# Queries that carry their softmax scale, one engine for the normalisation, a shorter feed-forward loop, and another order ahead of the expert gathers

## The chip, the cores and the metric

The kernel runs on one core of one Trainium2 chip. The metric is the device time of one execution in microseconds (us), median of three runs. The engines of a core are TensorE (PE; its weight loads are PEld), VectorE (DVE), ScalarE (ACT), GpSimd (POOL) and SyncE (SP), and 16 DMA engines move data. Each engine works through a queue of its own in order; they meet only at semaphores.

## What is computed

Two transformer-like blocks of two layers each, on 256 tokens of width 1024, everything in float32. Cut to what bears on this change:

```python
# first block, for each of 2 layers
h = rms_norm(x, mix_pre_gain[l])            # 16 heads of 64, from h @ w_in[l]:
o_a = neighbourhood attention  (4 heads "na": scores * 64**-0.5 + bias, softmax)
o_b = latent attention         (4 heads "mla": scores * 96**-0.5, softmax)
o_c = axial-rope attention     (4 heads "ax": q, k rms-normed, scores * 64**-0.5, softmax)
o_d = sliding window with sink (4 heads "sw": scores * 64**-0.5, masked, softmax)
x = x + rms_norm(concat(o_a, o_b, o_c, o_d) @ w_out[l], mix_post_gain[l])
h = rms_norm(x, ffn_pre_gain[l])
u = conv over tokens (width 3) of h @ w_up[l]      # 1024 -> 2 * 2816
gate, val = split(u)
x = x + rms_norm((gelu(gate) * val) @ w_down[l], ffn_post_gain[l])

# second block, for each of 2 layers
xn = rms_norm_2(x, norm1_g[l])
x = x + mixing_sublayer(xn, ...)            # 6 stick-breaking heads, 6 mLSTM heads, 4 gating groups
xn = rms_norm_2(x, norm2_g[l])
q = xn @ peer_wq[l]                         # 8 heads, 2 sides, 128 wide
top 16 of 128 key scores on each side, top 16 of their 256 sums  -> idx, gate = softmax
x = x + sum over the 128 picks of a token of gelu(xn . u_tab[idx]) * gate * v_tab[idx]
```

The last line gathers, for each of 256 tokens, 128 rows of each of two tables (stored side by side, 8 KB a pick): 536.9 MB over both layers.

## The kernel before

**Splitting.** A float32 product is done as three products of parts: each operand is split into a high and a low part, high times high, high times low, low times high. These are the matmuls of L154, L155 and L156. ScalarE writes high parts by a cast, VectorE writes low parts by a subtraction.

**First block, attention (`mixing`).** Sixteen heads go through a pipeline in the order sw, mla, ax, na, four of each. For a head h, TensorE computes scores (256 by 256, as one PSUM bank of 128 x 512) in one of three `score_bank`s. VectorE's `scaled(h)` multiplies by the scale (L896) or, for the masked kinds na and sw, multiplies and adds the mask in one operation, both into the tile `s_sb` in SBUF, then takes the negated row maximum (L898). ScalarE takes two exps from `s_sb`, with sums (L764), into `p_sb`. VectorE's `probs(h)` takes the reciprocal of the sums (L911) and multiplies the first token half by it (L913), while GpSimd multiplies the second half (L705). TensorE's `turn(h)` waits for both (semaphores `att_probs` and `att_probs_pool`) and transposes the probabilities (L1022), then multiplies them with v. TensorE's scores for head h wait until VectorE has scaled head h-3, since that frees the bank. Before that, GpSimd computes the reciprocal root for the axial q and k in one helper call, and ScalarE copies the latent queries (`lat_up`).

**First block, feed-forward (`gated_ffn`).** 22 chunks j of w_up and w_down. For a chunk TensorE does up(j) (two halves of the sequence of products into banks 4 and 5), ScalarE takes u to SBUF (L466), VectorE convolves (L526), ScalarE takes the gelu (L476), VectorE gates and splits the product (L534 to L539), TensorE does down(j) into four banks that collect over all chunks. ScalarE (L448, L454) and VectorE (L510) split the loaded weights, in two buffers each. TensorE's order is up(1); then a loop of ten turns with up, down, up, down; and at the end up(22), down(21), down(22). `pe_early` (L403) raises the two counts that let ScalarE write the first weight parts; it runs behind the out product of attention. `sp_early` issues the first two loads of w_up (L380), of w_down and of the convolution's parameters; SyncE runs it (L1107) behind its wait for all values of attention. `after_mix` is the norm behind attention's out product (L227), and `mid` the norm ahead of the feed-forward. In ScalarE's and VectorE's queues the splits of the first weights (`act_early`, `dve_early`) stand ahead of both.

**Second block (`mixing_out`).** The end of the mixing sublayer for token half 1 is interleaved with the choice of experts for token half 0. The orders are written out by hand, one list of calls for each engine: TensorE L2039 to L2076, ScalarE L2145 to L2171, VectorE from L2350. Names: `turn_x` (L1992) transposes the normed tokens, `take_x` copies the transposes to SBUF, `queries` (L2015, 32 matmuls of 128x128 in one row of the timeline) and `key_scores` compute the choice's scores; `first_choice` (L2260) takes the top 16 of each side, `second_choice` (L2278) the top 16 of the sums, `numbers` (from L2294) the table rows, whose last instruction writes `picked`. `sb_values` and `ml_rows`, `ml_probs`, `ml_values` (L1950) belong to the stick-breaking and mLSTM heads; `magnitudes` and `logs` (Ln, and so a table load on ScalarE, L1757) belong to the stick-breaking weights. `y_squares`, `y_sums` (L2203), `y_root` (L165, GpSimd), `y_scaled` (L2217) norm the head outputs; `out(1, n)` is the out product of token half 1. GpSimd issues the gathers (L1938), each one row of picks (8 KB into each of 128 partitions, 1 MB) into a ring of slots. The first four slots are free early (they wait for the values of the heads); numbers 5 to 8 wait for out(1, 0), the others for out(1, 1). Then, row by row, VectorE forms the dot product (L2326), the diagonal (L2336), and TensorE adds the row (L2034).

## Time and profile before

| | |
|---|---|
| median of 3 runs | 2390.38 us (2387.23 to 2391.78) |
| profiled execution | 2389.33 us, of which the span is 2387.6 us |
| busy: TensorE | 2072.4 us (87%) |
| busy: VectorE | 1749.7 us (73%) |
| busy: ScalarE | 843.5 us (35%) |
| busy: GpSimd | 698.4 us (29%) |
| moved by DMA | 700.50 MB, mean 293 GB/s |
| mean granted clock of TensorE | 0.953 |

Of the span, the first block takes up to about 690 us (layer 1 up to 345), the second block the rest. In the second block, each layer begins with some 170 us of mixing and ends with a gather phase of about 620 to 650 us, in which the DMA engines are the busiest. Times in the rows below are microseconds from the start of the span. A row of a timeline tells the start, the duration, the engine, the line, the operation with its tiles and shapes, and how many instructions it joins; in brackets the idle time of the engine just ahead of it, and what ended that. A granted clock of 1.00 is TensorE's full 2.4 GHz, 0.50 is 1.2 GHz.

### The profile page before, as it was taken

Reading aid. Unit: us, or ns where it says so; the run is one execution under the profiler, and the core shown is the slowest. Engines: PE = TensorE matmul, PEld = TensorE weight load, DVE = VectorE, ACT = ScalarE, POOL = GpSimd, SP = SyncE. Lnnn points to the kernel's source line nnn. Section 1 sums busy time; section 2 is a strip of 40 time slices with the busy share of each in tenths; the row PEclk is TensorE's granted clock in tenths of the full one; section 3 lists DMA queues with packets and bytes.
Section 4 is the critical chain, followed back from the end, with each engine's and each line's share of the span. In section 5 each row is a group of like instructions: output and inputs, shape, how many; then the busy total and the mean of one; then the engine's idle time right before and its main releaser. Section 6 shows DMA issues by size and latency. Waiting matters only on the chain. (4 is left out here: it accounts for less than half of the span.)

```text
span 2387.6 us, 28061 instructions
## 1 busy us (share of the span) xinstructions
PE 2072.4 (87%) x8698; PEld 1341.1 (56%) x8698; DVE 1749.7 (73%) x4213; ACT 843.5 (35%) x2074; POOL 698.4 (29%) x631
## 2 busy tenths in 40 slices
PE   8999999999979889898878777699899997777776
PEld 6779977679969765454333332298745542332232
DVE  6857777677767667778787787576676778787875
ACT  6656655666647521111111111176211211111110
POOL 1200001200001044444444444110243444444441
PEclk9999999999989889999999999998799999999999
DMA  6254533335535359999999999754399999999996
GB/s 220 80 214 180 187 120 91 120 135 186 186 132 165 124 205 420 419 421 421 422 421 421 421 421 422 266 156 150 131 421 419 421 421 421 421 422 421 421 422 269
DMA packets 138668, 700.50 MB, mean 293 GB/s; under 512 B 14392, under 2 KB 40248, under 8 KB 66872
## 3 DMA queue, kind: packets, MB, share of 16 engines
q0 software_dynamic: 73728, 536.90, 54.3%
q1 hardware_dynamic: 64824, 162.22, 19.5%
q8 instruction: 52, 0.85, 0.1%
q14 instruction: 64, 0.52, 0.1%
HBM read 698.03 MB, written 1.05 MB: 293 GB/s over the span
## 5 line engine op out<-in xcount | busy, mean ns | idle before, releaser
L2034 PE MATMUL bank<-ARENA 128*128 128x512 f32 x2048 | 990.5, 630 | 219.2 <-DVE ARENA L2336 218.4
L2034 PEld LDWEIGHTS bank<-ARENA 128*128 128x128 f32 x2048 | 385.4, 198 | 802.9 <-DVE ARENA L2336 432.0
L2326 DVE CUSTOM_DVE_ANT_0 ARENA<-ARENA 128x1024 f32<-128x1024 f32 x512 | 626.2, 1223 | 271.6 <-DMA ARENA<-in_uv_rows,ARENA 264.5
L1938 POOL DMA_INDIRECT ARENA<-in_uv_rows,ARENA x512 | 586.4, 1145 | 710.8 <-PE bank L2034 638.6
L154 PE MATMUL bank<-PARTS,PARTS 128*128 128x256 f32 (+4 forms) x1488 | 488.5, 328 | 17.6 <-DVE PARTS L539 7.0
L155 PE MATMUL bank<-PARTS,PARTS 128*128 128x256 f32 (+6 forms) x1552 | 497.5, 321 | 0.0
L156 PE MATMUL bank<-PARTS,PARTS 128*128 128x256 f32 (+6 forms) x1552 | 497.1, 320 | 0.0
L2142 ACT ACTIVATE ARENA<-ARENA 128x1 f32<-128x1 f32 x512 | 104.0, 203 | 1049.0 <-DVE ARENA L2326 1048.3
L154 PEld LDWEIGHTS bank<-PARTS,PARTS 128*128 128x128 f32 x1488 | 286.7, 193 | 42.4 <-DVE PARTS L284 7.4
L155 PEld LDWEIGHTS bank<-PARTS,PARTS 128*128 128x128 f32 (+2 forms) x1552 | 298.5, 192 | 16.7 <-issue 1.0
L156 PEld LDWEIGHTS bank<-PARTS,PARTS 128*128 128x128 f32 (+2 forms) x1552 | 298.0, 192 | 17.0
L2336 DVE TENSOR_SCALAR ARENA<-CON,ARENA 128x128 f32<-128x128 f32 x512 | 176.7, 345 | 10.1 <-ACT ARENA L2142 5.1
L213 POOL TENSOR_SCALAR STAT<-STAT 128x1 f32<-128x1 f32 x8 | 4.5, 565 | 450.4 <-ACT ARENA L207 450.4
L526 DVE SCALAR_TENSOR_TENSOR ARENA<-ARENA 128x255 f32<-128x255 f32 x176 | 77.4, 481 | 79.5 <-ACT ARENA L470 71.2
L2015 PE MATMUL bank<-ARENA 128*128 128x128 f32 (+1 forms) x704 | 121.7, 334 | 0.0
L2015 PEld LDWEIGHTS bank<-ARENA 128*128 128x128 f32 x704 | 111.2, 203 | 17.7 <-issue 9.9
L504 DVE TENSOR_TENSOR PARTS<-ARENA,PARTS 128x512 fp32r<-128x512 f32 x176 | 109.5, 686 | 9.1 <-ACT PARTS L448 9.1
L448 ACT CAST PARTS<-ARENA 128x512 fp32r<-128x512 f32 x176 | 95.9, 629 | 10.6 <-PEq L403 10.4
L1341 DVE TENSOR_TENSOR PARTS<-ARENA,PARTS 128x384 fp32r<-128x384 f32 (+2 forms) x160 | 72.4, 485 | 36.9 <-ACT PARTS L1337 36.7
L335 DVE TENSOR_TENSOR PARTS<-ARENA,PARTS 128x512 fp32r<-128x512 f32 (+2 forms) x112 | 67.6, 635 | 28.5 <-ACT PARTS L331 28.1
L1337 ACT CAST PARTS<-ARENA 128x384 fp32r<-128x384 f32 (+2 forms) x160 | 68.9, 460 | 32.9 <-PE bank L156 31.0
L331 ACT CAST PARTS<-ARENA 128x512 fp32r<-128x512 f32 (+2 forms) x112 | 61.7, 578 | 42.5 <-PE bank L156 40.9
(258 smaller groups left out, 1919.2 us busy)
## 6 DMA issues: line engine op xcount, KB each, us to landing
ARENA<-in_w_up_tiles SPq DMA_DIRECT2D x44, 1024.0 KB, 5.9
ARENA<-in_w_down SPq DMA_DIRECT2D x44, 512.0 KB, 3.7
ARENA<-in_w_out SPq DMA_DIRECT2D x32, 512.0 KB, 4.2
ARENA<-in_wq_tiles SPq DMA_DIRECT2D x16, 1024.0 KB, 11.8
ARENA<-in_w_in SPq DMA_DIRECT2D x40, 384.0 KB, 3.6
ARENA<-in_w_in SPq DMA_DIRECT2D x24, 512.0 KB, 10.5
ARENA<-in_w_in SPq DMA_DIRECT2D x40, 256.0 KB, 2.9
ARENA<-in_uv_rows,ARENA POOLq DMA_INDIRECT x512, 22.5
```

What stands on the lines that cost most here:

```text
L154: mm(out_ap, w_hi, x_hi, start=start, stop=False, skip_group_check=True)
L155: mm(out_ap, w_lo, x_hi, start=False, stop=False, skip_group_check=True)
L156: return mm(out_ap, w_hi, x_lo, start=False, stop=stop, skip_group_check=True)
L448: nc.scalar.copy(up_hi[s][u], up_raw[s][:, u, :]).then_inc(s_("up_hi"), 1)
L504: nc.vector.tensor_tensor(up_lo[s][u], up_raw[s][:, u, :], up_hi[s][u], ALU.subtract).then_inc(s_("up_lo"), 1)
L526: last = nc.vector.scalar_tensor_tensor(c[:, to], u[:, frm], w, c[:, to], ALU.mult, ALU.add)
L1938: nc.gpsimd.indirect_dma_start(out=slot[i % SLOTS], out_offset=None, in_=table[:, :], in_offset=bass.IndirectOffsetOnAxis(ap=picked[:, t, ...
L2015: last = mm(to, w[:, k, :], x, start=(k == 0), stop=(k == KD - 1), skip_group_check=True)
L2034: last = mm(row_banks[t][n][:, :], diag[i % N_DIAG], slot[i % SLOTS][:, D + n * 512:D + (n + 1) * 512], start=(c == 0), stop=(c == NPICK - ...
L2142: nc.scalar.activation(gelu_dots[:, t, c:c + 1], dots[:, t, c:c + 1], ACT.Gelu_apprx_tanh).then_inc(S("gelu_ready"), 1)
L2326: v.tensor_tensor_reduce(u, u, xn[:, t, :], 1.0, 0.0, ALU.mult, ALU.add, dots[:, t, c:c + 1]).then_inc(S("dots_ready"), 1)
L2336: v.tensor_scalar(diag[i % N_DIAG], ident, gelu_dots[:, t, c:c + 1], gate[:, t, c:c + 1], ALU.mult, ALU.mult).then_inc(S("diagonal_ready"), 1)
```

## The change

1. *Attention.* The scale goes with the queries: the reciprocal root of the axial q is taken with `64 * eps` and an unscaled sum of squares, which makes it 64^-0.5 times as large (one more operation on GpSimd), and ScalarE multiplies the latent queries by 96^-0.5 where it copied them. The eight heads without a mask lose their scaling operation on VectorE; their maximum and their exps read the PSUM bank. VectorE multiplies both halves of the probabilities, GpSimd none, and TensorE waits for VectorE alone. The scores of head h wait for the exps of head h-3 where that one has no mask.
2. *Feed-forward.* The buffers of w_up and w_down are laid out anew. The first w_up loads are issued right behind SyncE's wait for all scores, the w_down loads where they were. The loop is one turn shorter, and the order at the end is up(20), down(19), up(21), up(22), down(20), down(21), down(22). The splits of the last w_down move: ScalarE's behind taking u(22), VectorE's behind the convolution of 22.
3. *Second block.* Three orders change: TensorE does ml_rows(4) ahead of turn_x(0) and sb_values(2), (3) behind key_scores(0); ScalarE does logs(4) ahead of take_x(0); VectorE does first_choice(0) ahead of ml_probs(4) and second_choice(0) ahead of y_sums(1).

```diff
-            up_raw_at, up_at = at, at + 4096
-            down_raw_at, down_at = at + 12288, at + 14336
+            up_raw_at, up_at = at + 12288, at + 4096
+            down_raw_at, down_at = at, (at + 16384, at + 2048)
...
-            def sp_early(sp):
+            def sp_up_early(sp):
                 for s in range(2):
                     load_up(sp, s, s)
+
+            def sp_down_early(sp):
+                for s in range(2):
                     load_down(sp, s, s)
...
-                with pe.Fori(0, NF // 2 - 1) as it:
+                with pe.Fori(0, NF // 2 - 2) as it:
                     up(1, it * 2 + 2)
                     down(0, it * 2 + 1)
                     up(0, it * 2 + 3)
                     down(1, it * 2 + 2)
+
+                up(1, NF - 2)
+                down(0, NF - 3)
+                up(0, NF - 1)
                 up(1, NF)
+                down(1, NF - 2)
                 down(0, NF - 1)
                 down(1, NF, stop=True)
...
                     gelu(s, j + 1)
+                    if j + 2 < NF:
+                        act_split_down(act, 1 - s, j + 2, 16 * ((j + 1) // 2 + 1))
                     if j + 1 < NF:
-                        act_split_down(act, 1 - s, j + 2, 16 * ((j + 1) // 2 + 1))
                         take_u(1 - s, j + 2, j + 1)
...
                     if j == NF - 2:
                         fill(act, 4, 6)
+                        act_split_down(act, 1 - s, NF, 16 * (NF // 2))
...
-                dve_split_down(dve, 1, NF)
                 fill(dve, 0, 4)
                 convolve(1, NF, NF - 1)
+                dve_split_down(dve, 1, NF)
                 gated(1, NF)
...
-                    pool_rstd(pool, STAT[:, 16:28], 1.0 / HD, 12).then_inc(s_("ax_rstd"), 1)
-                    for h in range(NHD):
-                        pool.wait_ge(s_("att_recip"), h + 1)
-                        nc.gpsimd.tensor_scalar(p_sb[:, h % 3, 1, :], p_sb[:, h % 3, 1, :], sums[:, h, 1:2], None,
-                                                ALU.mult).then_inc(s_("att_probs_pool"), 1)
+                    nc.gpsimd.tensor_scalar(ssC[:, :, 0:4], ssC[:, :, 0:4], 1.0, HD * EPS, ALU.mult, ALU.add)
+                    nc.gpsimd.tensor_scalar(ssC[:, :, 4:6], ssC[:, :, 4:6], 1.0 / HD, EPS, ALU.mult, ALU.add)
+                    pool.drain()
+                    nc.gpsimd.tensor_tensor(ssC, ssC, view(HALF[:, 0:12], (6, NT), (1, 6)), ALU.pow).then_inc(s_("ax_rstd"), 1)
...
-                        nc.scalar.copy(qb[:, t, :], bank[t][:, 0:384])
+                        nc.scalar.mul(qb[:, t, :], bank[t][:, 0:384], 96 ** -0.5)
...
-                            last = nc.scalar.activation(p_sb[:, h % 3, t, :], s_sb[:, h % 3, t, :], ACT.Exp,
+                            frm = s_sb[:, h % 3, t, :] if masked[h] else score_bank[h % 3][:, t * T:(t + 1) * T]
+                            last = nc.scalar.activation(p_sb[:, h % 3, t, :], frm, ACT.Exp,
...
-                        else:
-                            nc.vector.tensor_scalar(s, frm, sc, None, ALU.mult).then_inc(s_("att_scaled"), 1)
-                        dve.drain()
+                            s = s_sb[:, h % 3, :, :]
+                            dve.drain()
                         last = nc.vector.tensor_reduce(nmax[:, h, :], s, AX, ALU.max, negate=True)
...
-                        nc.vector.reciprocal(sums[:, h, :], sums[:, h, :]).then_inc(s_("att_recip"), 1)
-                        dve.drain()
-                        nc.vector.tensor_scalar(p_sb[:, h % 3, 0, :], p_sb[:, h % 3, 0, :], sums[:, h, 0:1], None,
-                                                ALU.mult).then_inc(s_("att_probs"), 1)
+                        nc.vector.reciprocal(sums[:, h, :], sums[:, h, :])
+                        dve.drain()
+                        for t in range(NT):
+                            last = nc.vector.tensor_scalar(p_sb[:, h % 3, t, :], p_sb[:, h % 3, t, :], sums[:, h, t:t + 1],
+                                                           None, ALU.mult)
+                        last.then_inc(s_("att_probs"), 1)
...
-                        if h >= 3:
-                            pe.wait_ge(s_("att_scaled"), h - 2)
+                        if h >= 3 and masked[h - 3]:
+                            pe.wait_ge(s_("att_scaled"), masked_until[h - 3])
+                        elif h >= 3:
+                            pe.wait_ge(s_("att_exp"), h - 2)
...
-                        pe.wait_ge(s_("att_probs_pool"), h + 1)
...
                                  ).then_inc(S(f"mix_post_{l}"), 16)
+                    up_down.sp_up_early(sp)
                     sp.wait_ge(*mixed.all_values)
-                    up_down.sp_early(sp)
+                    up_down.sp_down_early(sp)
...
+                    ml_rows(pe, 4)
                     turn_x(0)
-                    sb_values(2)
-                    sb_values(3)
-                    ml_rows(pe, 4)
                     queries(0)
                     suffix_sums(pe, 4)
                     key_scores(0)
+                    sb_values(2)
+                    sb_values(3)
                     ml_scores(pe, 4)
...
                     magnitudes(act, 4)
+                    logs(act, 4)
                     take_x(0)
                     ml_weight(act, 4)
-                    logs(act, 4)
...
+                    first_choice(0)
                     ml_probs(4)
-                    first_choice(0)
+                    second_choice(0)
                     y_sums(1)
-                    second_choice(0)
                     numbers(0)
```

## Rows read from the trace of the kernel before

**Rows 1.** The page's slices: GB/s moved by DMA, 40 slices of 59.7 us

```profile
GB/s 220 80 214 180 187 120 91 120 135 186 186 132 165 124 205 420 419 421 421 422 421 421 421 421 422 266 156 150 131 421 419 421 421 421 421 422 421 421 422 269
```

**Rows 2.** GpSimd's timeline: start, us, engine, line, tiles, count, [idle, its releaser]

```profile
853.58 2.91 POOL L165 TENSOR_TENSOR STAT<-STAT,HALF 128x16 f32<-128x16 f32 x1
...
860.45 1.21 POOL L1938 DMA_INDIRECT ARENA<-in_uv_rows,ARENA  x1 [3.96 <-DVE ARENA L2310]
...
872.90 1.38 POOL L1938 DMA_INDIRECT ARENA<-in_uv_rows,ARENA  x1 [7.51 <-PE bank L156]
```

**Rows 3.** Table by stage, 874 to 875: engines' busy us, granted clock, DMA share, GB/s

```profile
874.00:875.00 1.00, 1.00 (x6) 0.80 (x6) 0.92 (x2) 0.00 (x0) 0.70 (x2) 1.00 0.23 49
```

**Rows 4.** VectorE's timeline before the first layer's gathers

```profile
847.31 0.48 DVE L2260 MAX8 ARENA<-ARENA 128x8 f32<-128x128 f32 x2
...
850.87 1.22 DVE L2203 TENSOR_REDUCE STAT<-ARENA 128x16 f32<-128x1024 f32 x1 [0.29 <-ACT ARENA L2096]
...
853.06 0.42 DVE L2278 MAX8 ARENA<-ARENA 128x8 f32<-128x256 f32 x1
...
855.81 0.17 DVE L2294 TENSOR_SCALAR ARENA<-ARENA 128x16 uint32<-128x16 uint32 x1
...
859.40 0.16 DVE L2217 TENSOR_TENSOR STAT<-STAT 128x6 f32<-128x6 f32 x1
```

**Rows 5.** TensorE's timeline, second block, and one row of the table by stage

```profile
828.78 1.97 PE L1992 MATMUL bank<-CON,ARENA 128*128 128x128 f32 x8 [1.58 <-DVE ARENA L2247]
...
836.42 6.69 PE L2015 MATMUL bank<-ARENA 128*128 128x128 f32 x32
...
846.53 3.79 PE L1950 MATMUL bank<-ARENA 128*128 128x65 f32 x32
...
882.38 3.73 PE L2015 MATMUL bank<-ARENA 128*128 128x128 f32 x32
...
829.00:842.00 13.00, 13.00 (x55) 11.64 (x55) 2.31 (x4) 3.64 (x7) 0.00 (x0) 0.50 0.00 0
...
1690.86 5.77 PE L1950 MATMUL bank<-ARENA 128*128 128x65 f32 x32
```

**Rows 6.** ScalarE's timeline, second block, first layer

```profile
827.39 0.63 ACT L1752 ACTIVATE ARENA<-ARENA 128x512 f32<-128x512 f32 x1
...
837.69 1.28 ACT L1757 ACT_TABLE_LOAD   x1
```

**Rows 7.** Timeline of three engines, end of the first feed-forward

```profile
332.35 1.12 ACT L454 CAST PARTS<-ARENA 128x512 fp32r<-128x512 f32 x2
...
333.89 1.30 DVE L510 TENSOR_TENSOR PARTS<-ARENA,PARTS 128x512 fp32r<-128x512 f32 x2
...
337.11 0.59 ACT L466 COPY ARENA<-bank 128x512 f32<-128x512 f32 x1 [3.64 <-PE bank L156]
...
340.97 0.43 DVE L534 TENSOR_TENSOR ARENA<-ARENA 128x256 f32<-128x256 f32 x1 [0.48 <-ACT ARENA L476]
...
342.32 0.50 PE L154 MATMUL bank<-PARTS,PARTS 128*128 128x512 f32 x1 [2.50 <-DVE PARTS L539]
```

**Rows 8.** ScalarE's and VectorE's timeline behind attention; the L380 loads' time to landing

```profile
135.20 4.27 ACT L448 CAST PARTS<-ARENA 128x512 fp32r<-128x512 f32 x8 [5.21 <-PEq L403]
...
DMA to landing us min/median/max: 4.9/4.9/4.9
...
141.88 2.72 DVE L227 TENSOR_TENSOR ARENA<-bank,ARENA 128x512 f32<-128x512 f32 x4
```

**Rows 9.** Groups by form, 78 to 112: busy us, mean ns, idle before, releasers

```profile
L705 POOL TENSOR_SCALAR ARENA<-ARENA,STAT 128x256 f32<-128x256 f32 x14 | 14.9, 1062 | 36.9 <-DVE STAT L911 36.9
...
L1022 PE MATMUL bank<-CON,ARENA 128*128 128x128 f32 x52 | 8.3, 282 | 1.7 <-POOL ARENA L705 0.9 <-issue 0.8
...
L896 DVE TENSOR_SCALAR ARENA<-bank 128x512 f32<-128x512 f32 x8 | 5.5, 689 | 0.6 <-PE bank L156 0.6
...
L913 DVE TENSOR_SCALAR ARENA<-ARENA,STAT 128x256 f32<-128x256 f32 x14 | 5.0, 354 | 1.3
```

More of the change, by code:

```diff
@@ L369, in gated_ffn @@
             up_lo = [[parts(up_at + (4 * s + u) * 1024 + 512, 512) for u in range(4)] for s in range(2)]
-            down_hi = [[parts(down_at + (2 * s + u) * 1024, 512) for u in range(2)] for s in range(2)]
-            down_lo = [[parts(down_at + (2 * s + u) * 1024 + 512, 512) for u in range(2)] for s in range(2)]
+            down_hi = [[parts(down_at[s] + u * 1024, 512) for u in range(2)] for s in range(2)]
+            down_lo = [[parts(down_at[s] + u * 1024 + 512, 512) for u in range(2)] for s in range(2)]
             g_hi = [parts(g_at + s * 512, T) for s in range(2)]
@@ L678, in mixing @@
                 nsink = STAT[:, 104:108]
-                scale_of = {"na": HD ** -0.5, "mla": 96 ** -0.5, "ax": HD ** -0.5, "sw": HD ** -0.5}
+                masked = [kind in ("na", "sw") for kind, *_ in heads]
+                masked_until = [sum(masked[:h + 1]) for h in range(NHD)]
                 score_bank = [bank[6], bank[7], bank[1]]
@@ L1043, in projected @@
                             if n == 0:
-                                pe.wait_ge(s_("att_scaled"), NHD - 1)
+                                pe.wait_ge(s_("att_scaled"), masked_until[NHD - 2])
                             if n < KD:
```

14 lines of the change are left out of this document (6 added, 8 removed).

## The prediction

> **What bounds the kernel now.** I read four views in this order. First the page's forty slices: from slice 16 to 25, and from 30 to the end, the DMA engines move 420 GB/s without a dip [rows 1]. These are the two gather phases of the second block (512 rows of 1 MB); nothing the change does alters their bytes, so each phase lasts as long as before and only its start can move. Second, GpSimd's timeline before the phase: the first gather goes out at 860.45 us, directly behind VectorE's write of `picked`, three follow it, and the fifth waits until 872.90 for out(1,0) on TensorE [rows 2]. Between them DMA falls to a share of 0.23 at 874 [rows 3]. So a microsecond won on the chain to the gathers is a microsecond won at the end, if the second batch moves along with the first. Third, the timelines of the three engines on that chain. Fourth, the first block: it has no transfer bound. TensorE sets its pace except in a few named gaps, so only those gaps can be won.
>
> **Part 1, VectorE order before the gathers.** In the kernel before, VectorE runs first_choice(0) (from 847.31), then y_sums(1) (850.87), second_choice(0) (853.06) and numbers(0) (855.81), whose last instruction writes `picked` at 859.49, just as y_scaled(1) begins (859.40) [rows 4]. y_sums(1) waited for TensorE's last values. The change puts second_choice(0) in front of y_sums(1). It lasts from 853.06 to the start of numbers(0) at 855.81, 2.75 us, and now runs while TensorE finishes the values, provided that the key scores come early enough (part 2 sees to that). After y_sums only numbers(0) is left: 859.49 − 855.81 = 3.7 us, of which 0.4 is a pause. GpSimd's y_root(1) stands ahead of the gathers in its queue: it begins 0.1 us behind y_sums and its pow ends at 856.49 [rows 2], 3.4 us after y_sums, so the two finish together. I take **2.9 us** a layer (2.75, plus the pause that overlaps), between 2.4 (GpSimd last) and 3.1. y_scaled(1) moves by as much, so out(1,0) and the second batch do too.
>
> **Part 2, TensorE order before the gathers.** Before: turn_x(0) at 828.78 after 1.58 us idle; sb_values(2), (3) from 830.55; ml_rows(4); queries(0) at 836.42, 6.69 us long; then values(2 to 4) as 32 matmuls from 846.53 to 850.15 [rows 5]. ml_rows(4) now fills the idle 1.6 us ahead of turn_x(0), and queries(0) follow turn_x directly. The cover that is gone: sb_values hid the copies of the turned x. ScalarE takes its half behind logs(4), which brings a table load ahead of it: magnitudes end at 828.0 and a load is 1.28 us [rows 6]; with 0.63 for the Ln and 0.59 for the copy that is 830.6; VectorE's half ends at about the same time. That is a bubble of 0.9 us. Net, the same matmuls end 0.7 us earlier at equal clock. The order also decides what waits: ml_probs(4) now stands behind first_choice(0) on VectorE, and ml_values(4), sb_values(4) wait for it. first_choice lasts 3.4 us, and over that time TensorE has sb_values(2), (3) (1.8 us at 2.4 GHz) and ml_scores(4) (1.8) to do, then ml_values(2), (3): covered.
> The unknown is the granted clock. From 829 to 842 it is 0.50, that is 1.2 GHz, after the 1.6 us of idle [rows 5]. With ml_rows(4) in the gap the engine is idle 0.4 and 0.9 us instead. At full clock a group of 32 query matmuls lasts 3.7 us (at 882.38), against 6.69 [rows 5], and turn_x 1.0 against 1.77. Working the whole chain at 2.4 GHz, y_squares' last part ends at 844.1 and y_sums starts then, not at 850.87: 6.7 us. With the clock falling where it falls now, y_sums starts at 848.5: 2.3 us. The second layer shows a third course: in its 32 value matmuls the clock fell with the engine busy, and they took 5.77 us, not 3.79 [rows 5]. The change puts 48 such narrow matmuls almost together. I take this middle course, the clock full through queries(0) and lost in the values: 6.7 − 1.9 = **4.8 us** in the first layer, and 7.1 − 1.9 = 5.2 in the second, where the present chain is 0.4 longer. Bounds a layer: −4.5 (all of it at half clock) to 7.1.
> A rule speaks against the order on ScalarE. The row shows the Ln starting 1.29 us after its table load starts, hence 1.28 a load [rows 6]. The Trainium skill, "ScalarE: Activation LUTs", section "What ACT_TABLE_LOAD costs", gives about 2.66 us for each switch, drain included. By it the copy of x, and the gathers, would come 1.4 us later a layer; the trace disagrees, so the row's figure stands.
> Sum of parts 1 and 2: 7.7 + 8.1 = **15.8 us**.
>
> **Part 3, the end of the feed-forward.** Before, the order is up(22), down(21), down(22). ScalarE takes u at 337.11, VectorE convolves, ScalarE takes the gelu, VectorE gates from 340.97, and TensorE idles 2.50 us until 342.32 [rows 7]. A down product lasts 2.75 us (twelve matmuls, 0.229 apart). Now down(20) comes behind up(22), so up(22) ends at 334.15 and two down products, until 339.65, cover the chain. But the split of the last w_down is moved into that chain: ScalarE may start it only when down(20) is done (337.1), 1.12 us for two casts, and the gelu stands behind it (338.3); VectorE splits from 337.8 in 1.3 us, then gates 1.35 us. Those durations are in [rows 7]. Product 22 can start at 340.5, a gap of 0.8 us. Gain 2.5 − 0.8 = 1.7 us a layer, **3.4 us**, from 0 to 5.0. up(22) is needed 2.75 us earlier; its low parts are written about 5 us before its present start, so it doesn't wait.
>
> **Part 4, earlier loads of w_up.** They move from the last values to the last scores, 14 us earlier. VectorE's post-norm starts at 141.88, 2.6 us after TensorE is done, because the splits of w_up precede it; that looks like a late load. It isn't: ScalarE's first cast at 135.20 was released by TensorE's sequencer at L403, `pe_early`, which the change leaves where it is, and the load issued at 125.44 had landed 4.9 us later, at 130.3, so ScalarE (idle from 129.98) had it [rows 8]. **0 us**. In between there is nothing that queues behind the two loads on SyncE's queue but the w_down loads, which start when they did.
>
> **Part 5, attention.** Per head without a mask VectorE loses a 512-wide scale from PSUM (0.69, with its drain 0.78 us) [rows 9]; every head gets a second 256-wide multiply (0.27 from start to start, 0.35 long [rows 9]). GpSimd's half took 1.06 us and released the transposes; the second multiply ends 0.44 us sooner (0.27 + 0.35 behind the first's start) [rows 9]. But TensorE is at its own pace: in 78 to 112 us it waited 1.7 us ahead of its transposes [rows 9], so 1.7 is the most to win a layer. Following the heads: the first two come 0.5 earlier, the MLA and axial ones run at TensorE's 2.34 and 2.50 us, the four neighbourhood heads keep their masked scale, get 0.27 us each and need 2.8 to 3.1 us of VectorE, so lag returns at the end. I take 0.6 a layer, **1.2 us**, from −0.5 to 1.7 each. The max and exps now read PSUM: the PSUM-reading L896 takes 689 ns [rows 9], the 512-wide SBUF reduction 686, so 0. The Trainium skill, "VectorE: DVE Perf Modes", section "The TRN2 errata", lists 62 more cycles for a PSUM source, an estimate of 0.065 us on eight heads a layer, 0.5 us; the two rows don't show it. The epsilon operation added on GpSimd (0.35 us) has 3.4 us until VectorE needs its result: 0.
>
> **Sum.** 15.8 + 3.4 + 0 + 1.2 = 20.4 us off the profiled execution: span 2387.6, whole 2389.3, so 2368.9. The median of the runs is 1.05 above the profiled one: **2370.0**.
>
> **Rivals.** *The clock stays at 2.4 GHz through the chain*: 9.6 + 10.0 in parts 1 and 2, 24.2 in all, 2366.2; the hole in DMA [rows 3] may close as well, about 1.2 us a layer, down to 2363. For it: the idle is shorter. Against: the narrow matmuls. *The clock falls ahead of queries(0), as now*: 5.2 + 5.0, 14.8 in all, 2375.6. For it: both layers did so. *The early loads do count*: post-norm starts at once, 2.2 us a layer more, 2365.6; [rows 8] speak against it. *The gathers don't follow the chain* (the parts' gains are lost in the waits between batches): 4.6 in all, 2385.8; the unbroken 420 GB/s speaks against it. *Slower*: with queries and 48 narrow matmuls in one piece, TensorE is held at 1.2 GHz from turn_x(0) through out(1,0). y_sums then starts 4.5 us later, less 2.9 for part 1, and out(1,0)'s 24 matmuls, 0.427 us apart instead of 0.227, take 10.2 us where 13 slow ones among them make 8.0 now: 3.8 later a layer, 7.6 against 4.6 won elsewhere: 2393.4. It decides from 2.3 us of lateness a layer on, about 11 us more at half clock than now.
>
> **How the numbers follow.** Forecast 0.36, clock stays 0.20, clock falls as now 0.24, loads count 0.05, gathers don't follow 0.07, slower mechanism 0.06, and 0.02 for things unseen. Two runs within 0.2% (4.8 us) can hardly be told apart. Faster by more: 0.36 + 0.20 + 0.24 + 0.05 + 0.01 = 0.86. Within: 0.07 + 0.03 of the slower case (it lies at +3) = 0.10. Slower by more: 0.04. The range takes the first four cases and the bounds of parts 3 and 5 (about ±2): 2362 to 2380.
>
> **What would show it.** First gathers at about 849 and 1695 on the old time axis, less what came before, with second_choice ahead of y_sums; granted clock 1.00 through queries(0) and 0.50 in the values; a gap near 0.8 us ahead of the last down product; ScalarE's first w_up cast still released by L403, with the post-norm 2.6 us behind TensorE. Wrong if the clock follows another course (±5 us), or if the start of the gathers moves and the end doesn't.

## The result, and the profile after

The changed kernel took **2375.69 us** (median of 5 runs, 2373.18 to 2378.83) against 2390.24 (5 runs) before: ratio 0.9943, interval 0.9929 to 0.9957, 14.6 us faster. In a second comparison it took 2379.38 (5 runs, 2374.26 to 2383.57) against 2390.27: ratio 0.9948, 0.9935 to 0.9962, 10.9 us faster. The profiled execution is one at 2378.83 us, span 2376.7, 10.9 us less than the span before. The forecast was 2370.0, a gain of 20.4, in a range of 2362 to 2380. So sign and range held, and part of the gain didn't come: 5.8 us of 20.4 by the first comparison, 9.5 by the second and by the profiled execution.

"Half clock" below is a granted clock of 0.50; a figure between 0.50 and 1.00 is the mean over a stretch that has both. First, the two slice rows of the page after the change, TensorE's granted clock and DMA's GB/s (40 slices of 59.4 us):

```profile
PEclk9999999999989889999999999998799999999989
...
GB/s 221 114 171 181 185 136 86 131 124 185 185 142 166 124 231 419 420 421 421 421 421 421 421 421 421 261 156 151 153 420 419 421 421 421 421 421 421 421 421 268
```

The gather phases are as they were, 420 GB/s from slice 16 to 25 and again from slice 30 on: only their start moved. So the question is where 10.9 us came from ahead of them. Subtracting the same instruction's start in the two traces gives this ledger. A minus sign is a gain.

| up to | shift of the start | gained in this stretch | forecast |
|---|---|---|---|
| last transposes of attention, layer 0 (121.01 to 120.53) | −0.48 | −0.5 | −0.6 |
| norm behind feed-forward 0 (345.37 to 344.26) | −1.11 | −0.6 | −1.7 |
| last transposes of attention, layer 1 (463.12 to 461.36) | −1.76 | −0.65 | −0.6 |
| norm behind feed-forward 1 (688.67 to 685.36) | −3.31 | −1.55 | −1.7 |
| turn_x(0), second block, layer 0 (828.78 to 825.44) | −3.34 | 0 | 0 |
| y_sums(1) (850.87 to 846.78) | −4.09 | **−0.75** | **−4.8** |
| first gather (860.45 to 853.31) | −7.14 | **−3.05** | −2.9 |
| end of the gather phase (1538.36 to 1530.63) | −7.73 | −0.6 | 0 |
| turn_x(0), layer 1 (1674.72 to 1668.74) | −5.98 | +1.75 | 0 |
| y_sums(1), layer 1 (1697.19 to 1690.04) | −7.15 | **−1.17** | **−5.2** |
| first gather, layer 1 (1706.63 to 1696.43) | −10.20 | **−3.05** | −2.9 |
| end of the gather phase (2380.71 to 2369.86) | −10.85 | −0.65 | 0 |

The row that failed is TensorE's chain from turn_x to y_sums. Its timeline in the first layer, which answers to [rows 5]:

```profile
825.44 1.97 PE L2007 MATMUL bank<-CON,ARENA 128*128 128x128 f32 x8 [0.20 <-DVE ARENA L2262]
...
828.24 5.73 PE L2030 MATMUL bank<-ARENA 128*128 128x128 f32 x32 [0.83 <-issue]
...
835.55 1.90 PE L1965 MATMUL bank<-ARENA 128*128 128x64 f32 x16
...
839.13 7.09 PE L1965 MATMUL bank<-ARENA 128*128 128x65 f32 x32
...
855.07 1.10 PE L1988 MATMUL bank<-CON,ARENA 128*128 128x128 f32 x8 [2.49 <-DVE ARENA L2238]
```

Turn_x is reached after 0.20 us of idle time instead of 1.58, as meant, and the bubble ahead of queries(0) is 0.83 us (0.9 in the forecast). But turn_x (1.97 us) and most of queries(0) (5.73 us, against 3.73 at full clock [rows 5]) run at half clock, and the 32 value matmuls take 7.09 us, twice their 3.79 [rows 5]. In the second layer it is the same:

```profile
1682.39 7.09 PE L1965 MATMUL bank<-ARENA 128*128 128x65 f32 x32
```

The table by stage shows why; the columns after the length are busy time and number for PE, PEld, DVE, ACT, POOL, then granted clock, DMA share and GB/s:

```profile
832.00:839.00 7.00, 6.94 (x54) 6.58 (x53) 3.32 (x17) 1.28 (x3) 0.00 (x0) 0.98 0.01 2
...
839.00:846.00 7.00, 7.00 (x34) 6.93 (x34) 3.47 (x13) 0.80 (x2) 0.00 (x0) 0.51 0.00 0
...
825.00:870.00 45.00, 39.69 (x200) 35.64 (x199) 28.56 (x99) 12.09 (x30) 10.59 (x9) 0.73 0.30 107
```

From 832 to 839 TensorE was busy 6.94 of 7.00 us at a clock of 0.98, and in the next seven it was busy throughout and had 0.51. So the clock fell in unbroken work: ahead of the fall stood the 64-wide sb_values (835.55) and ml_scores(4), whose matmuls use 64 rows. The same stretch of 45 us in the kernel before, and then, for each of the two kernels, the chain from turn_x to y_sums alone (before, after):

```profile
825.00:870.00 45.00, 35.49 (x203) 31.57 (x204) 23.96 (x83) 12.67 (x30) 7.69 (x7) 0.73 0.16 59
...
828.78:850.87 22.09, 22.03 (x121) 20.18 (x122) 6.88 (x23) 7.59 (x14) 0.00 (x0) 0.69 0.00 1
```

```profile
825.44:846.78 21.34, 20.45 (x114) 19.64 (x115) 9.23 (x34) 6.72 (x14) 0.00 (x0) 0.66 0.00 1
```

0.73 over the 45 us in both, and on the chain itself 0.69 before and 0.66 after: 13.6 us at half clock before, in one piece in turn_x to queries(0) (828.9 to 842), and 14.5 after, in two pieces (turn_x and queries(0), then the values). In the second layer it is 15.1 and 14.5. So the new order took no half clock off this chain, it only moved it from some of the work to other work. What is left is the 0.7 us that the prediction gave the order at equal clock (ml_rows(4) off the chain, the bubble on it): 0.75 was measured.

VectorE and GpSimd behind it (answering to [rows 4] and [rows 2]):

```profile
840.18 0.42 DVE L2293 MAX8 ARENA<-ARENA 128x8 f32<-128x256 f32 x1
...
846.78 1.22 DVE L2218 TENSOR_REDUCE STAT<-ARENA 128x16 f32<-128x1024 f32 x1 [3.94 <-ACT ARENA L2111]
...
848.96 0.17 DVE L2309 TENSOR_SCALAR ARENA<-ARENA 128x16 uint32<-128x16 uint32 x1
...
852.11 0.23 DVE L2325 TENSOR_SCALAR ARENA<-ARENA 128x16 uint32<-128x16 f32 x1
```

```profile
849.49 2.91 POOL L165 TENSOR_TENSOR STAT<-STAT,HALF 128x16 f32<-128x16 f32 x1
...
853.31 1.21 POOL L1953 DMA_INDIRECT ARENA<-in_uv_rows,ARENA  x1 [0.91 <-DVE ARENA L2325]
...
866.02 1.20 POOL L1953 DMA_INDIRECT ARENA<-in_uv_rows,ARENA  x1 [7.70 <-PE bank L156]
```

second_choice(0) (840.18) is done while TensorE works on the values. From the start of y_sums (846.78) to the first gather (853.31) it is now 6.53 us instead of 9.58: 3.05 us, in both layers. GpSimd's pow ends at 852.40 and VectorE's last instruction ends at 852.34, so they finish together, as forecast.

ScalarE's order (answering to [rows 6]):

```profile
824.73 1.28 ACT L1772 ACT_TABLE_LOAD   x1
...
826.03 0.63 ACT L1772 ACTIVATE ARENA<-ARENA 128x512 f32<-128x512 f32 x1
...
826.59 0.59 ACT L2129 COPY ARENA<-bank 128x512 f32<-128x512 f32 x1
```

The Ln starts 1.30 us after its table load, and the copy of x comes 0.56 us later: the row's 1.28 us held, not the 2.66 us of the Trainium skill ("ScalarE: Activation LUTs", section "What ACT_TABLE_LOAD costs").

The tail of the first feed-forward (answering to [rows 7]): ScalarE's split of the last w_down, and the first matmul of down(22).

```profile
338.00 1.14 ACT L463 CAST PARTS<-ARENA 128x512 fp32r<-128x512 f32 x2 [0.42 <-PE bank L156]
...
341.21 0.50 PE L154 MATMUL bank<-PARTS,PARTS 128*128 128x512 f32 x1 [0.58 <-DVE PARTS L550]
```

The gap ahead of down(22) is 0.58 us instead of 2.50, in the second layer too: 1.92 us each (forecast 1.7). Behind attention (answering to [rows 8]):

```profile
134.72 4.27 ACT L457 CAST PARTS<-ARENA 128x512 fp32r<-128x512 f32 x8 [5.21 <-PEq L407]
...
141.40 2.71 DVE L227 TENSOR_TENSOR ARENA<-bank,ARENA 128x512 f32<-128x512 f32 x4
```

The first cast of w_up is still released by TensorE's sequencer, 5.21 us late, and the norm starts 0.48 us earlier, by what attention won, no more: the early loads gave nothing. And attention, 78 to 112 us (answering to [rows 9]):

```profile
L1036 PE MATMUL bank<-CON,ARENA 128*128 128x128 f32 x53 | 8.9, 287 | 1.1 <-DVE ARENA L925 1.0
...
L925 DVE TENSOR_SCALAR ARENA<-ARENA,STAT 128x256 f32<-128x256 f32 x28 | 8.6, 350 | 1.1
...
L909 DVE TENSOR_REDUCE STAT<-bank 128x2 f32<-128x512 f32 x8 | 5.5, 687 | 1.6 <-PE bank L156 1.6
```

VectorE multiplies 28 halves at 350 ns each; TensorE waited 1.1 us ahead of its transposes instead of 1.7; the maximum read from PSUM takes 687 ns, from SBUF 686. The 62 more cycles that the Trainium skill ("VectorE: DVE Perf Modes", section "The TRN2 errata") gives a PSUM source don't show.

What ate the first block's gain in these two traces is the clock again. Rows before and after of the first product of the feed-forward, and before of the last down product of the second layer:

```profile
153.00:157.00 4.00, 3.98 (x33) 4.00 (x34) 2.23 (x6) 1.52 (x5) 0.00 (x0) 1.00 0.07 23
...
685.00:689.00 4.00, 3.63 (x10) 2.33 (x8) 0.33 (x1) 0.33 (x1) 0.00 (x0) 0.57 0.00 0
```

```profile
153.00:157.00 4.00, 4.00 (x23) 4.00 (x22) 1.72 (x5) 1.02 (x3) 0.00 (x0) 0.57 0.01 4
```

Behind the norm, the stretch at half clock lasted until 153 before and until 156.4 after: 1.3 us lost, and 1.8 in the second layer (until 494 and until 498). This is not the change's doing as far as the other traces show: the old first block stands unchanged in e1, e5 and e6 below, and its stretch lasts 3.4 or 6.8 us there (3.4 and 3.4, 3.4 and 6.8, 6.8 and 3.4 in the two layers); the new one stands in e4, e7, e8, e9 and e12, with 6.8 and 6.8, three times 6.8 and 3.4, and 3.4 and 3.4. On the other side, the 2.5 us gap in the second layer's tail was followed by 3.4 us at half clock (0.57 over 685 to 689); in the trace after there is none, a gain of 1.4 us that the forecast didn't have. In all the traces together, such a stretch follows the gap in five of ten places where the gap is 2.5 us (before, e1, e3, e5, e6, two layers each) and in none of 18 where it is 0.58, so closing the gap wins this part on average, not each time.

### The profile page after: what moved, and what is told of

It is laid out like the page before. It is cut to its first block and busy times, and to the rows that moved or that the text cites. A ratio compares the mean times of both kernels' runs of the same rounds, so it can differ in the third digit from the quotient of the medians.

```text
span 2376.7 us, 27988 instructions
## 1 busy us (share of the span) xinstructions
PE 2080.6 (88%) x8693; PEld 1345.2 (57%) x8698; DVE 1747.3 (74%) x4229; ACT 842.3 (35%) x2074; POOL 659.2 (28%) x601
```

## The experiments

**Each part alone, and the whole once more.** Four kernels; the kernel before took 2390.27 us in this comparison.

The second block's three orders alone:

```diff
  kernel before, and of the change only:
+                    ml_rows(pe, 4)
                     turn_x(0)
-                    sb_values(2)
-                    sb_values(3)
-                    ml_rows(pe, 4)
                     queries(0)
...
+                    logs(act, 4)
                     take_x(0)
...
+                    first_choice(0)
                     ml_probs(4)
+                    second_choice(0)
                     y_sums(1)
```

> The kernel before with the new orders of the second block alone (TensorE, ScalarE, VectorE). Theory A, the trace of the changed kernel read as it stands: from the write of y_sums to the first gather 3.05 us a layer are won (second_choice out of the way), from turn_x to y_sums only 0.75 and 1.17 us, because the granted clock falls again in the value matmuls; the hole in DMA shrinks by 0.6 us a layer. Sum 3.8 + 0.6 + 4.2 + 0.6 = 9.2 us faster: about 2381. In its trace the 32 value matmuls last near 7.1 us in both layers (3.79 and 5.77 before). Theory B, the fall in the values was an accident of that one execution, as the place of a clock fall moves with all that runs ahead of it: then at least one layer shows the 32 value matmuls in under 5.8 us, and the gain is 11 to 16 us.

Measured: 2380.29 us, ratio 0.9961 (0.9948 to 0.9973), 10.0 us faster; theory A had said 9.2. queries(0) and the values:

```profile
833.68 5.68 PE L2015 MATMUL bank<-ARENA 128*128 128x128 f32 x32 [0.83 <-issue]
...
844.54 7.09 PE L1950 MATMUL bank<-ARENA 128*128 128x65 f32 x32
```

7.09 us to the hundredth, and in the second layer too; turn_x to y_sums takes 21.31 us in both. With the changed kernel's two traces and that of e10, the values last 7.09 us eight times in eight, so this fall goes with the program's order and theory B falls.

The feed-forward alone (its hunks of the diff, unchanged):

> The kernel before with the feed-forward's part alone (buffers, early w_up loads, one turn less, new order at the end). Theory A: the gap ahead of the last down product shrinks from 2.50 to 0.6 us in both layers, 3.8 us in all, and the loads give nothing (ScalarE's first w_up cast is still released by TensorE's sequencer): about 2386. Theory B: closing the gap also keeps the clock up in the last product of the second feed-forward (at half speed in the kernel before from 685 to 689), 1.5 us more: about 2385. Rival: the loads count, post-norm starts at once, 8 us faster.

Measured: 2385.88 us, ratio 0.9980 (0.9971 to 0.9989), 4.4 us faster, between A's 3.8 and B's 5.3. There is no stretch at half clock in the last product in its trace (3.10 us of VectorE's idle time ahead of the norm, not 4.55), as B says. But the next experiment keeps the gap of 2.5 us, and its trace has no such stretch either (3.10 us), so one trace doesn't decide between A and B. The rival, that the loads count, falls.

Attention alone:

> The kernel before with the attention's part alone (scale in the queries, VectorE normalises both halves). Theory A: 0.5 to 0.65 us a layer, 1.1 us in all, about 2389, which the comparison can hardly tell from no change; in the trace the last transposes of probabilities stand 0.5 us earlier in the first layer and 1.1 us in the second. Rival: the shift by 0.5 us changes where the clock falls ahead of the feed-forward (3.4 us at half clock behind the transposes of the norm before, 6.8 us in the changed kernel), then attention alone is 1.3 us a layer slower there and the kernel is 1.5 us slower than before in all.

Measured: 2391.10 us, ratio 1.0001 (0.9992 to 1.0009): no change. The last transposes come 0.61 and 1.44 us earlier, as theory A has it, but turn_x(0) comes at 828.89 (828.78 before): the gain is gone between the norm behind feed-forward 1 and turn_x, where 41 us ran at half clock and not 24. That isn't the attention's doing, since e4 shows the same two figures for two executions of one program. The rival's place (149 us) was wrong, with 3.4 us at half clock there, as before.

The whole:

> The changed kernel again. Its first profiled execution was 3.1 us above its own median. Theory A (the clock's course is set by the program): the same stretches at half clock as in the first trace, 6.8 us from 149 on and 17 us between turn_x and out(1,0), values at 7.1 us. Theory B (it differs from execution to execution): other lengths, and the span differs by that: per 3.4 us at half clock on the chain, 1.7 us of time. Ratio to before 0.994 either way.

Measured: 2379.38 us; the profiled execution took 2383.57. Theory A held on the chain from turn_x to y_sums: queries(0) 5.63, values 7.09, 21.31 us in all. The 6.8 us at half clock from 149 came again too, but e9, with the same first block, has 3.4 there. But its turn_x(0) is at 829.29, 3.9 us later than in the first trace, with the norm behind the feed-forward at 685.52 (685.36). One row of each between the two, first this kernel, then the first trace:

```profile
795.00:813.00 18.00, 16.66 (x71) 13.26 (x71) 13.48 (x34) 15.39 (x33) 3.11 (x2) 0.53 0.66 259
```

```profile
795.00:813.00 18.00, 13.87 (x69) 10.80 (x69) 15.94 (x38) 16.67 (x38) 3.11 (x2) 0.72 0.58 229
```

0.53 against 0.72. Between 686 and turn_x this execution had 41 us at half clock, the first trace 24. So theory B holds for the stretches ahead of turn_x: they differ between executions of one program. The traces of e7, e8, e9 and e12, whose programs are the changed kernel up to turn_x, have 31 to 34 us there. This costs the one execution 3.7 us against the other, and so it is a large part of what can spread the changed kernel's ten runs over 10 us; only two of the ten left a trace.

Sum of the parts: 10.0 + 4.4 − 0.8 = 13.6, between the whole's 14.6 and 10.9. They add up.

**Which order gives what.** VectorE's order alone on the kernel before (only the first_choice and second_choice lines of the diff above):

> The kernel before with VectorE's new order alone (first_choice ahead of ml_probs(4), second_choice ahead of y_sums(1)); TensorE and ScalarE as before. Theory A (part 1 of the forecast is worth its 3 us only because TensorE brings the key scores earlier): first_choice starts no earlier, so ml_probs(4), which TensorE waits for, moves back behind it, and second_choice pushes y_sums back; picked is no earlier, and y_scaled(1) with the second batch is as late or later: 0 to 3 us slower a layer, 2390 to 2396. Theory B (the 3 us are VectorE's own): first gather 3 us earlier a layer, 2384.

Measured: 2385.88 us, ratio 0.9982 (0.9973 to 0.9991), 3.9 us faster. Theory A falls, and B's 6 us is too much:

```profile
853.78 3.68 PE L1950 MATMUL bank<-ARENA 128*128 128x65 f32 x16 [0.68 <-DVE ARENA L2192]
...
858.01 1.22 DVE L2203 TENSOR_REDUCE STAT<-ARENA 128x16 f32<-128x1024 f32 x1 [1.72 <-ACT ARENA L2096]
```

y_sums to the first gather is 6.82 us (9.58 before), so the 2.8 us are VectorE's own. But y_sums comes 23.30 us behind turn_x, not 22.09: TensorE waits 0.68 us for ml_probs(4), and 16 of its values run at half clock. From turn_x to the first gather that is net 1.5 and 1.9 us a layer.

TensorE's and ScalarE's orders alone (the other two hunks):

> The kernel before with TensorE's and ScalarE's new orders alone; VectorE as before. Theory A: from turn_x to y_sums 0.8 to 1.2 us less, the 32 value matmuls at half clock (7.1 us); VectorE's first_choice is done in time, but second_choice stays behind y_sums, so the first gather gains only that: 1 us a layer and some 0.3 of the hole, 2388. Theory B: the two orders are worth their sum only together (9.2 us), and this one alone nothing: 2390. Either way the values last 7.1 us.

Measured: 2385.04 us, ratio 0.9985 (0.9976 to 0.9993), 4.7 us faster.

```profile
843.91 6.50 PE L1950 MATMUL bank<-ARENA 128*128 128x65 f32 x32
```

Values 6.50 us, turn_x to y_sums 20.75 (1.3 to 1.7 less than before), y_sums to the gather 9.58 as before. Neither theory: it is worth about as much as VectorE's order, and within the intervals the two add up (3.9 + 4.7 = 8.6, of 10.0).

**What lets the clock fall in the values.** First, sb_values(2), (3) put back between turn_x and queries in the changed kernel:

```diff
                     turn_x(0)
+                    sb_values(2)
+                    sb_values(3)
                     queries(0)
                     suffix_sums(pe, 4)
                     key_scores(0)
-                    sb_values(2)
-                    sb_values(3)
                     ml_scores(pe, 4)
```

> The changed kernel with sb_values(2), (3) back between turn_x(0) and queries(0), all else as changed. Theory N (the clock falls in the values because 16 narrow value matmuls and the narrow ml_scores stand right ahead of them): the 32 value matmuls last 3.8 us again, and y_sums would come 3.3 us earlier but for VectorE, which gets the key scores about 1 us later and has 6.9 us of work ahead of y_sums: from turn_x to y_sums 19.7 to 20.5 us instead of 21.3, 1 to 1.6 us a layer faster than the changed kernel. Rival R (the clock falls a fixed time after turn_x, whatever the order): values at 7.1 us again, and the kernel the same or 1 us a layer slower than the changed one. Rival S (with sb_values there the half clock of the start lasts 13.7 us, as in the kernel before): queries(0) at 6.5 us, values 3.8, turn_x to y_sums about 22.3 us, 1 us a layer slower.

Measured: 2373.92 us, ratio 0.9931 (0.9913 to 0.9949).

```profile
840.62 2.00 PE L1965 MATMUL bank<-ARENA 128*128 128x65 f32 x16
...
843.54 3.68 PE L1965 MATMUL bank<-ARENA 128*128 128x65 f32 x16 [0.92 <-DVE ARENA L2207]
```

Half of the values ran full (2.00 us for 16), half at half clock. Turn_x to y_sums is 21.84 us, 0.5 more than in the changed kernel; the first half clock lasted 10.2 us. None of the three came out as written: the second fall came 17.0 us behind turn_x and not 13.7, which refutes a fixed time, and it came behind ml_scores and 16 values, so that narrow work precedes it here as well. It came inside the 0.92 us in which TensorE waited for VectorE, though, so that here a wait is as near a cause as the narrow work. The time can't be told from the changed kernel's.

Next, matmuls of zeros, 512 wide in bf16, whose result nobody reads, added to the changed kernel's work:

```diff
                     turn_x(0)
+                    wide(bank[2], 3)
                     queries(0)
                     suffix_sums(pe, 4)
                     key_scores(0)
+                    wide(bank[0], 2)
                     sb_values(2)
+                    wide(bank[0], 2)
                     sb_values(3)
+                    wide(bank[0], 4)
                     ml_scores(pe, 4)
```

where wide(to, n) is n times `matmul(to, ZERO[:, 0:P], ZERO[:, :])`.

> The changed kernel with 512-wide bf16 matmuls of zeros, whose result nobody reads, set between the steps: 3 behind turn_x(0), 2 ahead of sb_values(2), 2 ahead of sb_values(3), 4 ahead of ml_scores(4). At full clock they take 0.22 us each, 1.8 us for the eight. Theory N (narrow work lets the clock fall): the clock stays full through the values (3.8 us instead of 7.1), turn_x to y_sums is 21.3 + 1.8 + 0.4 - 3.3 = 20.2 us, 1 us a layer faster than the changed kernel. Rival R (the fall comes at a fixed time after turn_x, or from something else): the values stay near 7 us and y_sums is 2 us or more later: 2 to 4 us a layer slower.

Measured: 2368.46 us, ratio 0.9915 (0.9901 to 0.9930).

```profile
825.92 1.49 PE L2056 MATMUL bank<-ZERO 128*128 128x512 bf16 x3
...
827.20 3.86 PE L2030 MATMUL bank<-ARENA 128*128 128x128 f32 x32
...
837.89 3.79 PE L1965 MATMUL bank<-ARENA 128*128 128x65 f32 x32
```

The three fill the 0.83 us bubble and overrun it by 0.24 (at half clock they take 1.3 us), queries(0) run full, and so do the values: 18.07 us from turn_x to y_sums instead of 21.34, and 17.91 instead of 21.30 in the second layer. Theory N's sign is right, its sum too small, since it had not seen the first stretch shrink (6.8 to 3.4 us). Then the eight without the three:

> The changed kernel with the eight 512-wide matmuls of zeros behind key_scores(0) alone (2, 2 and 4, around the narrow value matmuls), without the three behind turn_x(0). With all eleven, turn_x to y_sums was 18.07 us instead of 21.34, queries(0) 3.86 instead of 5.73, the values 3.79 instead of 7.09. Theory N (each fall answers to the narrow work right ahead of it): the first stretch at half clock is 6.8 us again and queries(0) 5.6 to 5.8, the values stay at 3.8, turn_x to y_sums is 19.5 to 20 us: some 1.5 us a layer faster than the changed kernel. Rival (the first stretch sets the second): with the first as long as before, the values fall again, 7 us, and the eight cost their 1.8: 2 us a layer slower than the changed kernel.

Measured: 2375.95 us, ratio 0.9938 (0.9925 to 0.9952).

```profile
826.59 5.61 PE L2030 MATMUL bank<-ARENA 128*128 128x128 f32 x32 [0.83 <-issue]
...
839.03 5.67 PE L1965 MATMUL bank<-ARENA 128*128 128x65 f32 x32
```

Values 5.67 and 5.08 us, turn_x to y_sums 21.47 and 21.01: the eight alone win on the values what they cost. Theory N falls in this form, the rival holds more of it. And the three without the eight:

> The changed kernel with the three 512-wide matmuls of zeros behind turn_x(0) alone, without the eight. Of the four combinations, none and the eight alone have the first stretch at half clock 6.8 us long (queries(0) 5.6 to 6.2 us) and turn_x to y_sums 21.0 to 21.5 us, all eleven 3.4 us long, queries(0) 3.86 and 18.07 us. Theory P (the three set the first stretch, and with it the rest): queries(0) at 3.9 us, the values at 3.8 without the eight too, turn_x to y_sums 16.3 us; about 2366. Theory N' (the three shorten the first stretch, the narrow work ahead of the values still lets the clock fall a second time): queries(0) 3.9, values 5.5 to 7.1, turn_x to y_sums 18.2 to 19.8: about 2370. Rival (the three alone do nothing): queries(0) 5.7, 21.3 us, as the changed kernel.

Measured: 2368.54 us, ratio 0.9914 (0.9900 to 0.9928).

```profile
827.02 3.86 PE L2030 MATMUL bank<-ARENA 128*128 128x128 f32 x32
...
836.04 5.78 PE L1965 MATMUL bank<-ARENA 128*128 128x65 f32 x32
```

Theory N': queries 3.86 us (4.59 in the second layer, where the 3.4 us at half clock reach into them), the values 5.78 and 5.04, turn_x to y_sums 18.39 and 17.73. Of the four combinations, none gives 21.34, the eight 21.47, the three 18.39, all 18.07: **three dummy matmuls in a wait of 0.83 us are worth 3 us a layer, and the eight nothing.** The times agree: 2368.54 and 2368.46 us with the three, 2375.69, 2379.38 and 2375.95 without. Shown is thus that the half clock behind turn_x answers to how TensorE fills the bubble. Not settled is the fall in the values: with the eight wide ones ahead of them it still came (e9), and with the three besides it did not. Narrow work stood ahead of each of these falls, but narrow work alone doesn't decide, and no run sets wide work of the computation itself in its place.

**The early loads.** In the changed kernel, the release of the w_up buffers ahead of the last ten units of attention's out product:

```diff
+                    pe.sem_inc(S(f"ffn_{l}_up_used"), 2)
                     projected(6, out.n_units)
...
             def pe_early(pe):
-                pe.sem_inc(s_("up_used"), 2)
                 pe.sem_inc(s_("down_used"), 2)
```

> The changed kernel with the release of the w_up buffers (TensorE's count up_used) ahead of the last ten units of the out product, behind the last values of attention, instead of behind the product. Theory (the early loads had no effect because ScalarE's split waited for that count and not for data): ScalarE's first w_up cast begins at about 129.6 instead of 134.7, VectorE's post-norm at 139 instead of 141.4, 2.3 us earlier; TensorE's gap behind its 7 us of filling matmuls shrinks from 3.2 to 0.9, and the stretch at half clock behind it (6.8 us) may go, up to 3.4 more: 2.3 to 5 us a layer, 4.6 to 10 in all, against the changed kernel. Rival (the splits are late for another reason): nothing.

Measured: 2371.89 us, ratio 0.9917 (0.9903 to 0.9930), 3.8 and 7.5 us below the changed kernel's two medians.

```profile
129.03 4.27 ACT L456 CAST PARTS<-ARENA 128x512 fp32r<-128x512 f32 x8
...
134.34 1.15 ACT L462 CAST PARTS<-ARENA 128x512 fp32r<-128x512 f32 x2 [1.05 <-PEq L407]
...
146.33 1.09 PE L293 MATMUL bank<-CON,ARENA 128*128 128x128 f32 x8 [0.99 <-DVE ARENA L278]
```

The cast starts at 129.03, the norm at 138.46 (141.40 in the changed kernel), TensorE's idle time behind its filling matmuls (32 matmuls of zeros, which stand there in the kernel before as well) is 0.99 us instead of 3.17, and there is no stretch at half clock at 149 or 491 at all; in the twelve traces without the early release there is one each time. The norm behind feed-forward 0 is at 339.87 instead of 344.26, and attention in layer 1 ends at 456.98 instead of 461.36. The theory holds: the wait was for a count, not for data. With the release early the early loads may matter after all, since the old ones would land at about 130.3 [rows 8], behind the cast's new start; no run has the one without the other.

**All of it together**, with more of the wide matmuls in TensorE's waits (14 ahead of turn_y(0), 10 ahead of turn_y(1), 28 behind the last feed-forward, 12 at the start of each layer of the second block):

> The changed kernel with the early release, the eleven wide matmuls, and more of them in TensorE's waits: 14 ahead of turn_y(0) (idle 4.1 us), 10 ahead of turn_y(1) (idle 2.5 to 4 us), 28 behind the last feed-forward and 12 at the start of each layer of the second block (idle 10.7 and 5.6 us). They do no work of the computation. If the clock falls because TensorE idles or does narrow work, the stretches at half clock of 10 to 17 us behind each of these waits go; what counts of them is what lies on TensorE's chain: estimated 5 us at the start of the second block, 3 to 5 at each turn_y(0), 1 to 2 at each turn_y(1), with 7 from the eleven and 5 to 10 from the release: 2340 to 2355 us. If the idle wasn't the cause, 2360 to 2365. If a filler is late for its wait, it costs at most 0.5 us each.

Measured: **2362.29 us**, ratio 0.9883 (0.9868 to 0.9898): 28 us faster than before, 13 to 17 faster than the changed kernel. The start of the second block and the chain to y_sums in it, then the first of these in the changed kernel:

```profile
685.00:710.00 25.00, 20.71 (x106) 18.59 (x107) 15.10 (x33) 15.09 (x34) 2.81 (x5) 0.86 0.84 272
...
820.00:838.00 18.00, 17.89 (x134) 16.57 (x134) 9.03 (x35) 4.67 (x11) 0.00 (x0) 0.94 0.01 2
```

```profile
685.00:710.00 25.00, 12.25 (x57) 11.30 (x56) 16.78 (x29) 14.16 (x34) 5.60 (x9) 0.73 0.64 219
```

0.86 against 0.73 there, and the mean clock of the span is 0.968 (0.952). But 2362.29 lies where the expectation put the case that idle time isn't the cause (2360 to 2365), and not at its 2340 to 2355: of the stretches at half clock at the filled waits, most got shorter and few went (6.8 us instead of 10.2 and 3.4 at the start of the block, 6.8 instead of 10.2 around turn_y(0), 6.8 as before at turn_y(1)). Nor did the fillers beside the eleven win time that can be seen. e10's 3.8 to 7.5 us and e8's 7.2 to 10.9 below the changed kernel make 11 to 18, all of the 13 to 17 here. From the norm behind feed-forward 1 to turn_x it is 140.6 us with them, and 140.1 to 143.8 in the traces without.

## Why the forecast was right in sign and too large

- **Part 1** (2.9 us a layer): 3.05 measured, in both layers. Right, with its reason. Its condition ("provided that the key scores come early enough") was half right: e5 has y_sums to the first gather 2.8 us shorter without part 2, but TensorE then waits for ml_probs(4), and net 1.5 to 1.9 us are left.
- **Part 2** (4.8 and 5.2): 0.75 and 1.17. This is the failed step, and it is 8.1 of the 9.5 us by which the profiled execution missed the sum. The step read "I take this middle course, the clock full through queries(0) and lost in the values". I had taken the fall at 829 for an answer to the 1.58 us of idle time, and thought that 0.20 us wouldn't cause it. The clock was at half from turn_x for 6.8 us all the same, and the values ran at half from first to last (7.09 us), worse than the 5.77 us of [rows 5]. What the step put at a gain of 4 us from the clock was nothing; the 0.7 us at equal clock came. The second rival ("falls ahead of queries(0), as now", 2.3 us a layer, 2375.6 in all) was right about the start and had no loss in the values. That the first median (2375.69) came out on its number is luck: the ledger of the profiled execution adds up to 10.9 us and not to its 14.8, and the second comparison gave 2379.38. That the range held is owed to its width, which had this rival in it. In the terms of the bound from −4.5 to 7.1, the truth lay in the lower half.
- **Part 3** (3.4): 3.8 in the gaps, and 1.4 more from the clock in the second layer's last product, less 1.3 and 1.8 from longer half clocks at the start of the two feed-forwards. Mechanism and size of the gap were right; the clock beside it wasn't counted, and differs between executions. The ledger's two rows add up to 2.2.
- **Part 4** (0): right, and for the reason given; e10 shows the converse, that moving the release wins what moving the loads couldn't.
- **Part 5** (1.2): 1.13 in the trace; alone it can't be measured (e3).
- **The second batch** moved along, as assumed: 12.45 us behind the first before, 12.71 after. The gather phase got 0.6 us shorter a layer, half of what the first rival gave it for the hole in DMA; but the hole is still there (a DMA share of 0.53 over 873.45 to 876.45 before and of 0.57 over 866.31 to 869.31 after), so where the 0.6 us come from stays open. Between the gather phase and turn_x of layer 1, 1.75 us were lost again: 20.5 us at half clock from 1631 on, where there had been 17.1 from 1641 on.
- **Slower** (held at half clock from turn_x through out(1,0)): its mechanism was real in part (queries, all values and queries(1)), but the 45 us around it had a mean clock of 0.73 before and after, so that no half clock was added. It never reached its point of decision, 11 us more.

## What to carry to other kernels

When an engine with a granted clock sits on the chain, cost a reordering at both levels and take the pessimistic one unless a row shows that very order at the upper level: here the half clock moved with the work and didn't vanish. Try a few wide dummy matmuls in a short wait of TensorE on the chain itself: three of them, which delayed the work behind them by 0.24 us, were worth 3.0 to 3.6 us a layer, while TensorE's reordering alone won 4.7 us in both layers together (e6). More of them elsewhere won nothing that can be seen (e9, e11), so measure each place by itself. Before moving a load earlier, look at what releases its first reader.

## What the runs showed of the hardware

- The clock can fall with TensorE busy all the time (6.94 of 7.00 us ahead of the fall at 839). The Trainium skill ("TensorE: Matmul & The Clock Gate", section "HAM oscillation — how this bites in real kernels") tells of falls that waits for DMA bring about; the trace shows some without a wait.
- Two executions of one program had 41 and 24 us at half clock between the same two instructions, some 140 us apart, and 3.7 us more time in the one. So a stretch at half clock that one trace shows belongs to the program only where several traces agree, as they do in the values (7.09 us eight times in eight) and at turn_x, where a stretch at half clock starts within 1 us in each of the traces.
- Three 512-wide matmuls, 1.3 us at half clock, shortened such a stretch from 6.8 to 3.4 us, six times in six (e8, e11 and e12, two layers each).
